# Feeding the first modulation of a two-block diffusion layer: VectorE sums one shift vector, the adaptive loads start earlier, the second shift's matmuls move

## The chip, the cores and the metric

One core of one Trainium2 chip. The time is device microseconds for one execution, the median of the runs shown. All data is float32; the heavy products are made of three passes over high and low parts.

## What is computed

The part that matters is the beginning of the first block: six modulation vectors come out of one product of `silu(c)` (1 x 1024) with `ada_w` (1024 x 6144, 25.2 MB), and shift and scale enter the pooling mixer.

```python
def modulate(h, shift, scale):
    return h * (1 + scale) + shift

def ada_mods(cond, w, b):
    mods = (jax.nn.silu(cond) @ w + b)[..., None, :]
    return jnp.split(mods, ADA_CHUNKS, axis=-1)

# first_block
sh1, sc1, g1, sh2, sc2, g2 = ada_mods(c, ada_w[i], ada_b[i])
u = modulate(rms_norm(x, mix_pre_g[i]), sh1, sc1)
y = pool_mixer(u, pool_w[j], pool_scale[j])      # (window mean - u) @ w, four groups of 256
x = x + g1 * rms_norm(y, mix_post_g[i])
f = conv_ffn(modulate(rms_norm(x, ffn_pre_g[i]), sh2, sc2), ...)
x = x + g2 * rms_norm(f, ffn_post_g[i])
```

After it come the feed-forward block and a second block (two linear-attention mixers), which the change doesn't touch.

## The kernel before

The kernel is written by hand in five streams, one for each engine, that are kept in step by named semaphores. x (512 x 1024) lies as four token tiles in `xres`. Everything before the first feed-forward product takes about 79 us; then TensorE runs products until the end.

**The adaptive weights.** `ada_w` is read in 24 units of 1 MB: unit u = 4j + n holds the rows 256n to 256n + 255 of vector j (0 shift, 1 scale, 2 gate, 3 second shift, 4 second scale, 5 second gate). They pass through six slots (`ADA_SLOTS`). SyncE's `ada_unit` issues them in the order of u, from line 333 on, with `pool_w` (two halves of 512 KB) behind unit 7 and the first feed-forward weights (`unit(0, ...)`, line 339) behind unit 13. Ahead of unit 0 it waits until x has landed (line 332); from unit 6 on it waits until TensorE has used the unit that held the slot (`ada_used`). TensorE's `ada_unit(j, n)` (line 1791) multiplies a unit by the columns of `c_col` in four column groups of 32, so that each of the four partial sums has one row group of a bank. `ada_sum(j)` on VectorE (line 1087) copies the bank to `ada_part`, and `mod_col` on TensorE (line 1807) adds the partial sums and turns the vector into a column for every block of 128 channels; `mod_col` on VectorE (line 1100) adds the bias. The last vector, the second gate, goes another way: VectorE's `gate_sum` (line 1226) adds 128 x 1024 products into `g2_acc` with one SCALAR_TENSOR_TENSOR for each k, and a matmul with ones adds over the partitions.

**Order on TensorE, lines 1782 to 1940.** `keep_busy(14, 2)`, four turns of the small rows, the rows of `pool_scale` and `mix_post_g` spread over the partitions (line 1879), `keep_busy(2, 4)`, the band sums (line 1889, 16 matmuls), units 0 and 1, `pool_block(0)` to `(3)` (line 1839: the window means of the normed x), units 2 and 3, `pool_block(4)` to `(7)`, `mod_col(0)`, units 4 to 7, `mod_col(1)`, unit 8, then the mixer product tile by tile: `mixed(0)` with the units 9 to 11 between its groups, `mixed(1)` with `mod_row(2, 0)` behind its first group, `mixed(2)`, `mixed(3)`; then units 12 to 15, `turn_normed(0)`, the first half of `mod_col(3)`, units 16 and 17, `turn_normed(1)`, the second half, units 18 and 19, `turn_normed(2)`, `mod_col(4)`, `turn_normed(3)`, `keep_busy(6, 3)` and the first feed-forward product (line 291).

**Order on ScalarE, lines 559 to 630.** `Silu` for `c_col`, four square sums of x, a square root, the four normed tiles (line 567), the eight `pooled` copies (571), the eight scalings with SC1 (575), then square sums and roots of y and of the new x tile by tile. The copy of vector 3's partial sums (line 611) stands behind `norm_scale(1)`.

**Order on VectorE, lines 1061 to 1172.** Four copies for `edge_band`, four copies of columns behind `c_silu`, `pool_scale_row` and `post1_row` (1077, 1079), the inverse root, `band_sums` (1085), `ada_sum(0)`, `mod_col(0)`, `ada_sum(1)`, `mod_col(1)`; then for cb = 0 to 7 `scale_weights` at cb 0 and 4 (1137) and one SCALAR_TENSOR_TENSOR each (1149), which writes what the mixer reads; `ada_sum(2)`, the gate row (1154) and the four tiles of norm, scaling and addition.

Of the kernel before, what the change touches and what calls it, by code (L numbers as in the profile page):

```python
# [69 lines left out]
def build(nc, a, out, debug=None):  # L70
# [53 lines left out]
    vec_rows = at("vec_rows", PH + 24 * KB, [D])  # L124
# [85 lines left out]
    with ExitStack() as ctx:  # L210
# [88 lines left out]
        def _(sp):  # L299
# [32 lines left out]
            sp.wait_ge(S("x_in"), 16 * TT)  # L332
# [138 lines left out]
        def _(act):  # L471
# [100 lines left out]
            act.wait_ge(S("mods_done"), 2)  # L572
# [35 lines left out]
            act.wait_ge(S("ada_used"), 16)  # L608
            act.wait_ge(S("mod_mm"), 2)
            act.wait_ge(S("ada_summed"), 3)  # L610
# [418 lines left out]
        def _(v):  # L1029
# [37 lines left out]
            v.wait_ge(S("rows_turned"), 1)  # L1067
            v.wait_ge(S("c_silu"), 1)
            V.tensor_copy(bgk_norm[:], ps[:, 6, KD:KD + LH + DV // P]).then_inc(S("cols_done"), 1)
            V.tensor_copy(conv_taps[:].rearrange("p a n -> p (a n)"), ps[:, 7, 16:16 + 8 * FC]).then_inc(S("cols_done"), 1)  # L1070
            V.tensor_copy(gdn_taps[:].rearrange("p a n -> p (a n)"), ps[:, 7, 16 + 8 * FC:16 + 8 * FC + P]).then_inc(S("cols_done"), 1)

            v.wait_ge(S("rows_turned"), 1)
            V.tensor_copy(cond_cols[:].rearrange("p a k -> p (a k)"), ps[:, 6, 14:62]).then_inc(S("cols_done"), 1)
            v.wait_ge(S("cols_done"), 4)
            v.wait_ge(S("vec_mm"), 1)
            V.tensor_copy(pool_scale_row[:], bank2(2)).then_inc(S("vec_done"), 1)
            v.wait_ge(S("vec_mm"), 2)
            V.tensor_copy(post1_row[:], bank2(0)).then_inc(S("vec_done"), 1)
# [7 lines left out]
            def ada_sum(j):  # L1087

                v.wait_ge(S("ada_used"), 4 * j + 4)
# [5 lines left out]
                else:  # L1095
                    if j == 4:
                        v.wait_ge(S("ada_summed"), 4)
# [1454 lines left out]
```

## Time and profile before

| | |
|---|---|
| median of 3 runs | 1148.26 us (1147.45 to 1153.53) |
| span of the profiled execution | 1146.0 us |
| TensorE busy | 1128.1 us (98%) |
| VectorE, ScalarE, GpSimd busy | 551.4, 503.3, 450.0 us |
| granted TensorE clock, mean | 0.995 |
| first feed-forward product starts | 79.08 us |

The one time that the trace gives for the profiled execution is its span, from the first to the last instruction; what lies around it is in the median alone, which is 2.3 us above. In the profile a matmul of float32 stands as several passes, so counts of TensorE lines are passes; "L291" is line 291; a queue's name with q (SPq, ACTq) is the issuing of its transfers; the bracket at a row's end is the engine's idle time just before it and what ended it.

### The profile page before, as it was taken

How to read it: one execution, taken by the hardware profiler on the slowest of the kernel's cores; microseconds unless marked ns; L12 is line 12 of the kernel's file. 1: busy time of each engine (PE TensorE's matmuls, PEld its weight loads, DVE VectorE, ACT ScalarE, POOL GpSimd, SP SyncE). 2: the span in 40 equal slices, each digit the busy share in tenths (PEclk: the TensorE clock that was granted, in tenths of full speed). 3: DMA queues.
4: the chain of work that ended last, by engine and by line, in shares of the span. 5: the costliest groups of instructions: out<-in, count | busy, mean ns of one | idle time of the engine just before them, and what ended most of it. 6: DMA issues, size and time to landing. Idle time of an engine off the chain costs nothing.

```text
span 1146.0 us, 17133 instructions
## 1 busy us (share of the span) xinstructions
PE 1128.1 (98%) x6818; PEld 920.9 (80%) x6818; DVE 551.4 (48%) x907; ACT 503.3 (44%) x701; POOL 450.0 (39%) x340
## 2 busy tenths in 40 slices
PE   9999999999999999999999999999999999999997
PEld 6568888888888888878788878888888888888886
DVE  2472554334452234577986655422200443676836
ACT  4474553544421223865443245745322343534632
POOL 0015544445455471654442311034454534564430
PEclk9899999999999999999999999999999999999999
DMA  9994232332342333424232211222243322323201
GB/s 347 413 360 132 74 110 77 106 110 73 110 126 79 110 110 112 148 86 136 74 88 98 74 37 38 74 74 74 96 137 110 110 79 82 103 75 112 74 1 74
DMA packets 86216, 128.97 MB, mean 113 GB/s; under 512 B 13300, under 2 KB 66306, under 8 KB 85895
## 3 DMA queue, kind: packets, MB, share of 16 engines
q1 hardware_dynamic: 80706, 119.62, 30.9%
q10 hardware_dynamic: 5445, 8.42, 2.1%
q8 instruction: 48, 0.79, 0.3%
q14 instruction: 17, 0.14, 0.0%
HBM read 122.77 MB, written 5.26 MB: 112 GB/s over the span
## 4 chain that ended last, share of the span: by engine, by line
PE 88%; DVE 6%; ACT 3%; DMA 1%; issue 1%; SPq 0%; POOL 0%; DVEq 0%; ACTq 0%; POOLq 0%
PE ps L291 24%; PE ps L293 23%; PE ps L292 23%; PE ps L1773 3%; DVE conv_v L1291 2%; PE ps L1854 1%; PE ps L1803 1%; PE ps L2244 1%; DVE diag L1352 1%; PE ps L2245 1%; PE ps L1779 1%; PE ps L2313 1%; PE ps L2303 1%; PE ps L2250 1%; DVE outer L1349 1%
## 5 line engine op out<-in xcount | busy, mean ns | idle before, releaser
L426 POOL TENSOR_TENSOR wl<-raw,wh 128x512 fp32r<-128x512 f32 x312 | 419.4, 1376 | 615.6 <-ACT wh L477 615.6
L291 PE MATMUL ps<-xth,wh 128*128 128x512 f32 (+1 forms) x832 | 324.6, 390 | 1.5 <-DVE xtl L1188 0.9
L293 PE MATMUL ps<-xth,wl 128*128 128x512 f32 (+1 forms) x832 | 317.5, 382 | 0.0
L292 PE MATMUL ps<-xtl,wh 128*128 128x512 f32 (+1 forms) x832 | 317.2, 381 | 0.0
L477 ACT ACTIVATE wh<-raw 128x2048 fp32r<-128x2048 f32 x78 | 149.3, 1914 | 303.9 <-PE ps L293 281.9
L291 PEld LDWEIGHTS ps<-xth,wh 128*128 128x128 f32 x832 | 156.5, 188 | 34.7 <-issue 4.4
L293 PEld LDWEIGHTS ps<-xth,wl 128*128 128x128 f32 x832 | 156.4, 188 | 30.4
L292 PEld LDWEIGHTS ps<-xtl,wh 128*128 128x128 f32 x832 | 156.7, 188 | 28.8 <-issue 0.5
L1196 DVE SCALAR_TENSOR_TENSOR conv_out<-ps,conv_taps,conv_out 128x511 f32<-128x511 f32 x44 | 32.8, 744 | 124.8 <-ACT conv_out L644 124.8
L1291 DVE SCALAR_TENSOR_TENSOR conv_v<-ps,gdn_taps,conv_v 128x511 f32<-128x511 f32 (+2 forms) x96 | 71.8, 748 | 38.2 <-ACT conv_v L712 35.5
L291 PE MATMUL ps<-wh,xth 128*128 128x512 f32 x176 | 69.7, 396 | 0.1
L293 PE MATMUL ps<-wh,xtl 128*128 128x512 f32 x176 | 68.5, 389 | 0.0
L292 PE MATMUL ps<-wl,xth 128*128 128x512 f32 x176 | 68.5, 389 | 0.0
L291 PE MATMUL ps<-wh,act_parts_h 128*128 128x512 f32 x160 | 62.4, 390 | 0.0
L293 PE MATMUL ps<-wh,act_parts_l 128*128 128x512 f32 x160 | 62.3, 389 | 0.0
L292 PE MATMUL ps<-wl,act_parts_h 128*128 128x512 f32 x160 | 62.2, 389 | 0.0
L1610 DVE SCALAR_TENSOR_TENSOR xres<-xres,ps 128x1024 f32<-128x1024 f32 x7 | 8.5, 1220 | 90.5 <-PE ps L293 90.5
L712 ACT ACTIVATE conv_v<-ps,gdn_taps 128x512 f32<-128x512 f32 x32 | 21.9, 683 | 54.7 <-PE ps L293 29.9
L291 PE MATMUL ps<-wh,ogt_h 128*128 128x512 f32 x112 | 43.8, 391 | 0.0
L293 PE MATMUL ps<-wh,ogt_l 128*128 128x512 f32 x112 | 43.6, 389 | 0.0
L292 PE MATMUL ps<-wl,ogt_h 128*128 128x512 f32 x112 | 43.6, 389 | 0.0
L1222 DVE CAST act_parts_h<-acts 128x512 fp32r<-128x512 f32 x20 | 9.9, 495 | 65.3 <-PE ps L293 65.3
(350 smaller groups left out, 1644.9 us busy)
## 6 DMA issues: line engine op xcount, KB each, us to landing
ada<-in_ada_w SPq DMA_DIRECT2D x24, 1024.0 KB, 11.3
raw<-in_gdn_w_in SPq DMA_DIRECT2D x24, 1024.0 KB, 5.2
raw<-in_ffn_w_up SPq DMA_DIRECT2D x22, 1024.0 KB, 4.9
raw<-in_gla_w_in SPq DMA_DIRECT2D x12, 1024.0 KB, 5.0
raw<-in_ffn_w_down SPq DMA_DIRECT2D x11, 1024.0 KB, 4.9
raw<-in_gdn_w_out SPq DMA_DIRECT2D x8, 1024.0 KB, 4.9
raw<-in_gla_w_out SPq DMA_DIRECT2D x4, 1024.0 KB, 5.0
xres<-in_x SPq DMA_DIRECT2D x4, 512.0 KB, 4.9
```

Of the source, the lines that this page charges most:

```text
L291: nc.tensor.matmul(o, lh, rh, start=first, stop=False)
L292: nc.tensor.matmul(o, lh, rl, start=False, stop=False)
L293: return nc.tensor.matmul(o, ll, rh, start=False, stop=last)
L426: rest = nc.gpsimd.tensor_tensor(lo[:, part], raw[:, s, part], hi[:, part].bitcast(f32), ALU.subtract)
L477: nc.scalar.activation(wh[:, s if w is None else w, :], raw[:, s, :], ACT.Copy).then_inc(hi_done, 1)
L712: nc.scalar.activation(conv_v[:, sub, :], ps[:, piece_bank(piece), :], ACT.Copy, scale=gdn_taps[:, 3, ch:ch + 1]).then_inc(S("tap3"), 1)
L1196: V.scalar_tensor_tensor(dst[:, 1:T], src[:, 0:T - 1], conv_taps[:, 0, ds(chunk, 1)], dst[:, 1:T], ALU.mult, ALU.add).then_inc(S("conv_lef ...
L1291: V.scalar_tensor_tensor(dst[:, j:T], src[:, 0:T - j], gdn_taps[:, 3 - j, ch:ch + 1], dst[:, j:T], ALU.mult, ALU.add)\
L1349: V.tensor_tensor(prod, diag[:, 0:j, j:j + 1].broadcast_to([P, j, n]), diag[:, j:j + 1, j + 1:32].broadcast_to([P, j, n]), ALU.mult).then_ ...
L1352: V.tensor_tensor(diag[:, 0:j, j + 1:32], diag[:, 0:j, j + 1:32], prod, ALU.add).then_inc(S("diag_done"), 1)
L1773: return X.transpose(o, x, ident[0:n, 0:n])
L1779: X.matmul(ps[:, b, 0:256], ones[:, 0:1].broadcast_to([P, P]), group_rows[:, 0:1].broadcast_to([P, 256]), start=True, stop=True)
```

## The change

- VectorE makes the first shift vector: `shift_sum(k)` multiplies a unit's half by `c_col[k]` and adds it into `shift_acc` (one TENSOR_SCALAR and seven SCALAR_TENSOR_TENSOR of 128 x 1024), and `shift_col` on TensorE adds over the partitions with eight matmuls of one column. TensorE's units 0 to 3, `ada_sum(0)` and their `mod_col(0)` are gone.
- SyncE no longer waits for x ahead of unit 0. Units 6 to 9 wait for `shift_summed`, later ones for `ada_used`, whose count is four lower. `unit(0, ...)` goes two units earlier.
- The turned rows share bank 0; `Silu` stands behind the first two square sums; the band sums come ahead of the spread rows on TensorE, `keep_busy(2, 4)` is gone, all eight `pool_block` follow each other, and then come units 4 to 7.
- VectorE's order is inverse root, `band_sums`, the two spread rows, the eight `shift_sum`, `scale_weights(0)`, `ada_sum(1)`, the scale column, the shift column. ScalarE scales with SC1 as soon as the scale column is there.
- TensorE calls `keep_busy(2, 7)` ahead of `mod_col(1)` and again behind `shift_col`. Unit 12 goes ahead of `mixed(2)`, unit 13 between its groups; units 14 and 15 stay behind `mixed(3)`.

```diff
-            sp.wait_ge(S("x_in"), 16 * TT)
...
-                if u >= ADA_SLOTS:
-                    sp.wait_ge(S("ada_used"), u - ADA_SLOTS + 1)
+                if u >= ADA_SLOTS + 4:
+                    sp.wait_ge(S("ada_used"), u - ADA_SLOTS - 3)
+                elif u >= ADA_SLOTS:
+                    sp.wait_ge(S("shift_summed"), 2 * (u - ADA_SLOTS) + 2)
...
-            for u in range(8, 14):
+            for u in range(8, 12):
                 ada_unit(u)
             unit(0, (0, w_up[0, 0]))
-            for u in range(14, 20):
+            for u in range(12, 20):
...
-            act.wait_ge(S("rows_turned"), 1)
-            nc.scalar.activation(c_col[:], ps[:, 6, 0:KD], ACT.Silu).then_inc(S("c_silu"), 1)
             for tt in range(TT):
                 act.wait_ge(S("x_in"), 16 * TT)
+                if tt == TT // 2:
+                    act.wait_ge(S("rows_turned"), 1)
+                    nc.scalar.activation(c_col[:], ps[:, 0, 0:KD], ACT.Silu).then_inc(S("c_silu"), 1)
                 square_sum(junk[:], xres[:, tt, :], stat[:, 0, tt:tt + 1])
...
-            act.wait_ge(S("mods_done"), 2)
+            act.wait_ge(S("mods_done"), 1)
...
+            def shift_sum(k):
+
+                u = k // 2
+                v.wait_ge(S("c_silu"), 1)
+                if k % 2 == 0:
+                    v.wait_ge(ada_full[u], 16)
+                if k == 0:
+                    V.tensor_scalar(shift_acc[:], ada[:, u, 0, :], c_col[:, 0:1], None, ALU.mult).then_inc(S("shift_summed"), 1)
+                else:
+                    v.wait_ge(S("shift_summed"), k)
+                    V.scalar_tensor_tensor(shift_acc[:], ada[:, u, k % 2, :], c_col[:, k:k + 1], shift_acc[:], ALU.mult, ALU.add)\
+                        .then_inc(S("shift_summed"), 1)
...
-            ada_sum(0)
-            mod_col(0, 2, SH1)
...
+            vector_rows()
+            for k in range(KD):
+                shift_sum(k)
+            scale_weights(0)
             ada_sum(1)
             mod_col(1, 3, SC1, PRE1)
+            mod_col(0, 2, SH1)
             v.wait_ge(S("mods_done"), 2)
-            v.wait_ge(S("cols_done"), 8)
             for cb in range(KD):
-                if cb % 4 == 0:
-                    scale_weights(cb // 4)
+                if cb == KD // 2:
+                    scale_weights(1)
...
+            def shift_col(b):
+
+                pe.wait_ge(S("shift_summed"), KD)
+                for k in range(KD):
+                    mm = X.matmul(ps[:, b, k:k + 1], shift_acc[:, k * P:(k + 1) * P], ones[:, 0:1], start=True, stop=True)
+                mm.then_inc(S("mod_mm"), 1)
+
+            pe.wait_ge(S("cols_done"), 8)
+            for cb in range(KD):
+                pool_block(cb)
             pe.wait_ge(S("vec_done"), 2)
-            ada_unit(0, 0)
-            ada_unit(0, 1)
-            pe.wait_ge(S("cols_done"), 8)
-            for cb in range(4):
-                pool_block(cb)
-            ada_unit(0, 2)
-            ada_unit(0, 3)
-            for cb in range(4, KD):
-                pool_block(cb)
-            mod_col(0, 2, 0)
-            mod_col(0, 2, 1)
             for n in range(4):
                 ada_unit(1, n)
+            pe.wait_ge(S("pooled_done"), KD)
+            keep_busy(2, 7)
             mod_col(1, 3, 0)
             mod_col(1, 3, 1)
+            shift_col(2)
+            keep_busy(2, 7)
             ada_unit(2, 0)
-            pe.wait_ge(S("pooled_done"), KD)
...
+            def second_shift(g):
+
+                if g == 1:
+                    ada_unit(3, 1)
+
             mixed(0, gate_unit)
             mixed(1, gate_row)
-            mixed(2)
+            ada_unit(3, 0)
+            mixed(2, second_shift)
             mixed(3)
-            for n in range(4):
-                ada_unit(3, n)
+            ada_unit(3, 2)
+            ada_unit(3, 3)
```

## Rows read from the trace of the kernel before

**Rows 1.** The page's first line

```profile
span 1146.0 us, 17133 instructions
```

**Rows 2.** The chain that ended last, 0 to 130 us: start, length, what

```profile
22.39 4.09 PE ps L1839 x32
...
53.03 9.50 PE ps L1854 x44
62.53 1.90 PE ps L1803 x16
64.44 7.28 DMA ada<-in_ada_w
```

**Rows 3.** Timeline of TensorE, 50 to 86 us

```profile
67.10 0.43 PE L1813 MATMUL ps<-group_rows,ada_part 128*32 128x1 f32 x32
...
71.76 1.06 PE L1803 MATMUL ps<-ada,c_col 128*32 128x512 f32 x8 [0.18 <-DMA ada<-in_ada_w]
...
75.35 2.78 PE L1779 MATMUL ps<-group_rows,ones 128*128 128x256 f32 x12
```

**Rows 4.** Timeline of ScalarE, 50 to 90 us

```profile
59.11 1.02 ACT L501 ACTIVATE junk<-ps 128x1024 f32<-128x1024 f32 x1 [0.82 <-PE ps L1854]
...
66.47 0.58 ACT L611 ACTIVATE ada_part<-ps 128x512 f32<-128x512 f32 x1
```

**Rows 5.** Windows: stretch, length, busy time (count) by engine, PEclk, DMA share, GB/s

```profile
35.00:38.50 3.50, 2.16 (x80) 0.89 (x72) 1.11 (x4) 0.09 (x1) 0.00 (x0) 1.00 1.03 416
38.50:42.00 3.50, 2.82 (x10) 1.03 (x11) 3.50 (x5) 3.50 (x6) 0.00 (x0) 0.51 1.03 421
42.00:45.40 3.40, 3.40 (x11) 1.90 (x14) 3.40 (x6) 1.43 (x3) 0.00 (x0) 0.50 1.02 418
```

**Rows 6.** Timeline of all engines, 0 to 125 us: ScalarE's part of it

```profile
6.71 1.28 ACT L560 ACT_TABLE_LOAD   x1 [6.71 <-issue]
...
12.17 1.05 ACT L501 ACTIVATE junk<-xres 128x1024 f32<-128x1024 f32 x1
...
17.06 1.28 ACT L509 ACT_TABLE_LOAD   x1
...
18.80 4.27 ACT L567 ACTIVATE xn<-xres,stat 128x1024 f32<-128x1024 f32 x4 [0.24 <-DVE stat L1050]
```

**Rows 7.** Timeline of ScalarE in the feed-forward loop, 100 to 118 us

```profile
105.59 1.28 ACT L477 ACT_TABLE_LOAD   x1
```

**Rows 8.** Timeline of all engines, 0 to 125 us: VectorE's part of it

```profile
15.22 1.21 DVE L1079 COPY post_row<-ps 128x1024 f32<-128x1024 f32 x1
...
18.80 2.48 DVE L1085 COPY band_sum<-ps 128x512 f32<-128x512 f32 x4
```

**Rows 9.** The source line of `gate_sum`

```profile
L1235 DVE SCALAR_TENSOR_TENSOR g_acc<-ada,c_col,g_acc x8: 1276/1285/1289, 132.8 to 157.7; 128x1024 f32<-128x1024 f32 x8
```

**Rows 10.** Timeline of SyncE's queue, 0 to 130 us

```profile
9.33 13.49 SPq L326 DMA_DIRECT2D ada<-in_ada_w  x8
```

**Rows 11.** The tile `ada`, 0 to 110 us: its transfers

```profile
DMA to landing us min/median/max: 5.1/11.3/15.9
```

**Rows 12.** The tile `pool_w`, 0 to 50 us: its transfers

```profile
L336 SPq DMA_DIRECT2D pool_w<-in_pool_w x1: 507/507/507, 23.4 to 23.4; - x1
...
DMA to landing us min/median/max: 11.3/11.8/12.4
```

**Rows 13.** Timeline of VectorE, 33 to 48 us

```profile
36.49 0.69 DVE L1098 COPY ada_part<-ps 128x512 f32<-128x512 f32 x1 [3.27 <-PE ps L1803]
...
38.41 1.22 DVE L1137 TENSOR_TENSOR pool_w<-pool_w,pool_scale_row 128x1024 f32<-128x1024 f32 x1
39.56 2.74 DVE L1149 SCALAR_TENSOR_TENSOR pooled<-band_sum,mod_cols,pooled 128x512 f32<-128x512 f32 x4
```

**Rows 14.** Timeline of TensorE, 33 to 52 us

```profile
37.23 0.71 PE L1813 MATMUL ps<-group_rows,ada_part 128*32 128x1 f32 x64 [0.79 <-DVE ada_part L1098]
38.63 1.93 PE L1803 MATMUL ps<-ada,c_col 128*32 128x512 f32 x8 [0.69 <-DMA ada<-in_ada_w]
41.11 3.75 PE L1854 MATMUL ps<-pool_w,pooled 128*128 128x256 f32 x8 [0.55 <-ACT pooled L575]
```

More of the change, by code:

```diff
@@ L1107, in mod_col @@
                     V.scalar_tensor_tensor(out, ps[:, b, 0:KD], 1.0, bias, ALU.add, ALU.add).then_inc(S("cols_done"), 1)
-                    v.wait_ge(S("cols_done"), 9 if which == SC1 else 12)
+                    v.wait_ge(S("cols_done"), 10 if which == SC1 else 12)
                     V.tensor_tensor(out, out, cond_cols[:, gain, :], ALU.mult).then_inc(S("mods_done"), 1)
@@ L1126, in turned_out @@
                               bank2(turned_bank(tt)).rearrange("p (k n) -> p k n", n=P)).then_inc(S("pooled_written"), 1)
-            inv_root(stat[:, 0, 0:TT], D, EPS, TT)
-            band_sums()
-            ada_sum(0)
-            mod_col(0, 2, SH1)
             def scale_weights(part):
@@ L1785, in _ @@
             pe.wait_ge(S("ident_in"), 16)
-            turn(ps[:, 6, 0:62], rows[0:62, 0, :], 62)
-            turn(ps[:, 7, 16:16 + 4 * FC], rows[0:4 * FC, 1, :], 4 * FC)
-            turn(ps[:, 7, 16 + 4 * FC:16 + 8 * FC], rows[0:4 * FC, 2, :], 4 * FC)
-            turn(ps[:, 7, 16 + 8 * FC:16 + 8 * FC + P], rows[:, 3, :]).then_inc(S("rows_turned"), 1)
+            turn(ps[:, 0, 0:62], rows[0:62, 0, :], 62)
+            turn(ps[:, 0, 64:64 + 4 * FC], rows[0:4 * FC, 1, :], 4 * FC)
+            turn(ps[:, 0, 64 + 4 * FC:64 + 8 * FC], rows[0:4 * FC, 2, :], 4 * FC)
+            turn(ps[:, 0, 64 + 8 * FC:64 + 8 * FC + P], rows[:, 3, :]).then_inc(S("rows_turned"), 1)
             def ada_unit(j, n):
@@ L1794, in ada_unit @@
                 pe.wait_ge(ada_full[u % ADA_SLOTS], 16 * (u // ADA_SLOTS + 1))
-                if n == 0 and j >= 2:
-                    pe.wait_ge(S("ada_summed"), j - 1)
-                    if j >= 3:
-                        pe.wait_ge(S("mods_done"), 3)
+                if n == 0 and j >= 3:
+                    pe.wait_ge(S("ada_summed"), j - 2)
+                    pe.wait_ge(S("mods_done"), 3)
                 for b in range(2):
@@ L1874, in turn_normed @@
                 turn_tile(xn[:, tt, :], turned_bank(tt))
-            pe.wait_ge(S("prepared"), 8)
-            for r, b in ((0, 2), (32, 0)):
-                for half in range(2):
-                    mm = X.matmul(ps[:, b + half, :], ones[r:r + 1, 0:1].broadcast_to([1, P]), vec_rows[r:r + 1, half * 512:half * 512 + 512],
-                                  start=True, stop=True)
-                mm.then_inc(S("vec_mm"), 1)
-            pe.wait_ge(S("c_silu"), 1)
-            pe.wait_ge(S("cols_done"), 4)
-            keep_busy(2, 4)
             pe.wait_ge(S("band_in"), 20)
@@ L1891, in _ @@
                 mm.then_inc(S("pool_mm"), 1)
-            pe.wait_ge(S("vec_done"), 2)
-            ada_unit(0, 0)
-            ada_unit(0, 1)
-            pe.wait_ge(S("cols_done"), 8)
-            for cb in range(4):
-                pool_block(cb)
-            ada_unit(0, 2)
-            ada_unit(0, 3)
-            for cb in range(4, KD):
-                pool_block(cb)
-            mod_col(0, 2, 0)
-            mod_col(0, 2, 1)
+            for r, b in ((0, 2), (32, 0)):
+                if r:
+                    pe.wait_ge(S("c_silu"), 1)
+                    pe.wait_ge(S("cols_done"), 4)
+                for half in range(2):
+                    mm = X.matmul(ps[:, b + half, :], ones[r:r + 1, 0:1].broadcast_to([1, P]), vec_rows[r:r + 1, half * 512:half * 512 + 512],
+                                  start=True, stop=True)
+                mm.then_inc(S("vec_mm"), 1)
+            def shift_col(b):
[6 more added lines that the diff above has]
+                pool_block(cb)
+            pe.wait_ge(S("vec_done"), 2)
             for n in range(4):
                 ada_unit(1, n)
+            pe.wait_ge(S("pooled_done"), KD)
+            keep_busy(2, 7)
             mod_col(1, 3, 0)
             mod_col(1, 3, 1)
+            shift_col(2)
+            keep_busy(2, 7)
             ada_unit(2, 0)
-            pe.wait_ge(S("pooled_done"), KD)
             def gate_unit(g):
@@ L1964, in _ @@
             pe.wait_ge(S("mods_done"), 5)
-            pe.wait_ge(S("ada_summed"), 5)
+            pe.wait_ge(S("ada_summed"), 4)
             up_units(0)
```

38 lines of the change are left out of this document (20 added, 18 removed).

## The prediction

> **What bounds the kernel now.** I read the page first: a span of 1146.0 us [rows 1], TensorE busy for 98% of it. From 79.08 us on, products of three passes follow each other and nothing that the change touches is in them, so the change is worth what it moves the moment 79.08, with its sign turned, and no more. The profiled span is 2.3 us below the median of 1148.26 us; I work out a shift against the span's clock and add it to the median.
>
> Then the chain of waits. It seems to give the answer at once: 7.28 us from 64.44 to 71.72 belong to the landing of an adaptive unit [rows 2]. The reader should not take that for a stall of 7.28 us. TensorE's timeline shows the unit used at 71.76 after 0.18 us of idleness [rows 3]; until then it had work that could not go earlier. That work began at 67.10 with the second shift's first half column, which needs `ada_part`, and ScalarE writes it in 66.47 to 67.05, behind its whole row of square sums and roots [rows 4]. That row is fed at 59.11 by a square sum that had waited 0.82 us for the mixer product: `mixed(2)` ends there, since seven groups at 9.50 / 11 = 0.86 us from 53.03 make 59.07 [rows 2, 4]. So the line that sets the end is: scale column, mixer product up to the end of `mixed(2)`, the ScalarE and VectorE row up to 67.05, units 16 to 19 and three turns, 79.08. The last transfer is beside it, 0.2 us late.
>
> The third view is the granted clock: 1.0 from 35 to 38.5 us with TensorE busy for 2.16 of 3.5, then 0.5 (the 1.2 GHz level) until 45.4, although it was busy for 2.82 of 3.5 and 3.40 of 3.40 [rows 5]. A unit's eight passes took 1.93 us there [rows 14] against 0.95 at full clock (16 in 1.90 [rows 2]).
>
> **The change, part by part.**
>
> *The start.* ScalarE can begin its square sums when x is there, 9.33 us, where SyncE's wait ends now [rows 10], instead of 12.17 [rows 6]. Two take 2.5 us, to 11.8. Then comes `Silu`. Now one table load stands ahead of it at 6.71 where nothing waits, and the square sums use the same table. Which table a kernel that starts with a square sum loads first, the trace doesn't show, but its feed-forward loop does show the pattern: a plain copy (line 477) loads a table that doesn't serve the Gelu after it, so each pass loads twice [rows 7]. I take it that the first square sum loads such a common table and `Silu` needs a second load in the middle: 1.28 us, bounds 0 and 1.28. `Silu` ends at 13.3, the square sums at 15.8 instead of 17.05, and with the second load of 1.28 the normed tiles begin at 17.6 instead of 18.80: 1.2 us gained. The Trainium skill (ScalarE: Activation LUTs, What ACT_TABLE_LOAD costs) prices a switch at 2.66 us, as a load and a drain of 1.38; by it the gain would be gone. The trace has the load at 17.06 for 1.28 us and its root right behind it, so I use the row [rows 6].
>
> *The transfers.* Without the wait unit 0 follows x directly, and units 0 to 5 are in by about 25 us. But unit 6 now waits for VectorE's second `shift_sum`. VectorE does `band_sums` (2.48 us) from 17.6 to 20.1 and two row copies of 1.2 us to 22.5 [rows 8]. The eight sums cost 1.285 us each in `gate_sum` [rows 9], 1.31 with the wait on themselves; the first is a TENSOR_SCALAR, bounded by 0.6 and 1.3, taken as 1.1. The second ends at 24.9, the fourth at 27.5, the eighth at 32.7. **So the shift vector is not summed as the units land, but as VectorE comes free.** Unit 6 is issued at 24.9 and lands 5.1 us later at the earliest [rows 11], at 30.0. At the 2.5 us for 1.05 MB that 416 GB/s make [rows 5], unit 7 is in at 32.5 and `pool_w` at 35.1. Now its second half, issued at 23.4, lands 11.8 us later, at 35.2 [rows 12]. The early start of the stream is lost in the gap behind unit 5. Behind `pool_w` nothing starves: unit 11 lands at 45, unit 13 at 53, unit 19 at 68, some 4 us ahead of now, which frees the 0.2 us of [rows 3].
>
> *The scale column.* `scale_weights(0)` stands ahead of `ada_sum(1)` and needs `pool_w`: 35.1 to 36.3. `ada_sum(1)` then ends at 37.0; now it ends at 37.18, and scaling starts at 38.4 [rows 13]. So the scale vector comes first in the order, but 0.2 us earlier in time. The 3.8 us of units 0 to 3 that TensorE no longer works are not on this line.
>
> *The shift column and the mixer.* What moves is the 1.2 us of `scale_weights(0)` [rows 13], which is over before SC1, and in its place stands `shift_col`. It is sixteen passes with 128 columns of weights and one of output. Bounds: `mod_col`'s 64 passes took 0.71 us [rows 14], 0.2 us for sixteen; `pool_block`'s passes, with as many weights and 144 columns, took 4.09 / 32 = 0.13 [rows 2], 2.0 us for sixteen, and twice that at half clock, 4.1. Between these I take 1.3 us, since the weights are the dear side's and the output the cheap side's. TensorE is at 37.7 after `mod_col(1)`, at 39.0 after `shift_col`; VectorE's mixing products begin at 39.3 (39.56 now [rows 13]). Then TensorE has four passes of `keep_busy` (0.93 us at 2.78 / 12 [rows 3], 1.85 at half clock) and unit 8, which now runs in 38.63 to 40.56 while scaling goes on. `mixed(0)` begins at 40.9 at full clock, at 42.8 at half; now at 41.11 [rows 14]. Which clock? TensorE here idles more of the stretch ahead of 38.5 than it does now, and now the clock falls; once down it stayed there until 45.4 [rows 5]. I take the half clock, so `mixed(0)` is 1.7 us late. Its first two groups and half-clock tail repeat what now costs 3.75 us, but some of the delay is made up: 45.4 finds it in its second group, and from there on it is at full speed and doesn't wait for VectorE. Worked out group by group (two at half clock from 42.8 to 45.6, then two groups, three units and `mixed(1)`'s first group at 0.95 to 1.05 each) the gate row starts at 51.6 and 53.03 becomes 53.3: 0.3 us late. At full clock throughout the same count gives 51.1, 1.9 us early. With the dearest `shift_col` it is 2.0 us late; if the clock comes back at 42 instead of 45.4, 1.7 us early.
>
> *Units 12 and 13.* They cost 2 x 0.95 = 1.9 us [rows 2]. Now they run after 62.53, where TensorE would otherwise wait for 67.05. The change puts unit 12 ahead of `mixed(2)` and unit 13 in it, and the end of `mixed(2)` is on the line that sets the end: 59.07 becomes 59.07 + 0.3 + 1.9 = 61.3. The hole they leave ahead of 67 is filled by nothing. This is the largest term, a loss of 1.9 us, and the change gains only if the mixer starts more than that early.
>
> *The rest.* From the second tile's square sum on, everything is shifted; unit 19's 0.2 us come back. The first feed-forward unit lands 5 us earlier, and it is not late now.
>
> **The sum**: 0.3 + 1.9 - 0.2 = 2.0 us later. The median becomes 1148.26 + 2.0 = **1150.2 us**.
>
> **The rivals.**
>
> *The clock holds.* The two `keep_busy` calls keep 2.4 GHz over the mixer's start. For: that is work just where the clock falls. Against: 0.93 us each, when 2.16 in 3.5 did not hold it [rows 5]. The term is -1.9 instead of 0.3, with the other two -0.2: 1148.1 us. If in addition `Silu` shares the first table, 1.3 us more: 1146.8. Together 22%.
>
> *The chain's transfer is a true stall.* Then a last unit that lands 4 us earlier moves 79.08 by nearly that: 1148.26 - 3.7 = 1144.6. For it speaks the chain [rows 2], against it the 0.18 us [rows 3]. 8%.
>
> *The hole at 65 us.* TensorE, done with units 14 and 15, turns a tile and then waits some 1.5 us for `ada_part`. If that brings the clock down, units 16 to 19 and the turns run at half: four units at 0.98 more and two of the turns' 1.0, about 4 us on top: 1154.2, slower. [...] 12%. The Trainium skill (TensorE: Matmul & The Clock Gate, Part 4: PE-mode transpose) says that a transpose doesn't count as busy; by that rule this rival would be likelier. No row shows it.
>
> *The change doesn't do what it says at its start.* The adaptive units, now right behind x, share the transfer engines with the small rows and `pool_band`; band sums start late, VectorE with them, unit 6 with VectorE. With 2 us there: 1152.2. Against: the small rows compete with x already. 8%.
>
> The rest, 50%, is the forecast, with its bounds 1148.3 (the clock back at 42) and 1152.0 (the dearest `shift_col`).
>
> **How the numbers follow.** The forecast's own bounds, the clock rival and the late start make 1146.8 to 1152.2; that leaves out the transfer rival and the clock's fall at 65 us. Range 1146.5 to 1153.0. A measurement of this kernel tells about 0.5% (5.7 us) from no change: under 1142.5 or over 1154.0. No case reaches the first except a sum of the best ones, 3%; the hole's 1154.2 lies on the second, and half of it with a little for mishaps makes 7%; same 90%.
>
> **What would show it.** Right: a second table load ahead of `Silu` near 11.8; first `shift_sum` near 22.5, with units 0 to 3 long landed; a gap in the transfers near 25 us; `ada_sum(1)` ending near 37; clock 0.5 from about 38.5 to 45; `mixed(2)` ending near 61.3, line 611's copy near 69, no wait for unit 19, and the first product near 81. Wrong: full clock over 38 to 45; a first product before 79; a clock below 1.0 after 60; or a span that differs from that moment's shift, for then something in the later stages answers to the earlier transfers.

## The result and the profile after

The changed kernel takes 1156.70 us (median of 6 runs, 1154.00 to 1158.28) against 1148.12 us of the kernel before (6 runs): a ratio of 1.0075, with a 95% interval of 1.0063 to 1.0087. It is slower, 8.6 us by the medians. The forecast was 1150.2 us with a range of 1146.5 to 1153.0: the sign was right, the size four times too small, and the result outside the range. It also lies above 1154.0 us, which the forecast had given 7%.

The profiled execution has a span of 1152.4 us and a time of 1154.18 us. The page's first line and its row of busy times:

```profile
span 1152.4 us, 16995 instructions
...
PE 1126.2 (98%) x6742; PEld 920.7 (80%) x6742; DVE 559.4 (49%) x914; ACT 504.2 (44%) x702; POOL 450.1 (39%) x340
```

The span is 6.4 us longer than in [rows 1], and the first feed-forward product starts at 85.87 instead of 79.08, 6.8 us later. In both kernels 1066.5 to 1066.9 us lie between that product and the end, so the loss is all made before it. Where, the chain that ended last tells; its part up to 42 us, with start, length and what it was:

```profile
5.62 10.13 DMA pool_band<-in_pool_band
16.76 5.99 PE ps L1897 x32
22.75 1.92 PE ps L1905 x8
...
25.84 1.21 DVE post_row L1082
27.05 0.67 DVE shift_acc L1091
27.83 1.30 DVE shift_acc L1094
29.25 1.29 DVE shift_acc L1094
30.63 1.30 DVE shift_acc L1094
32.87 7.09 DMA pool_w<-in_pool_w
39.99 1.22 DVE pool_w L1149
41.21 0.61 DVE ada_part L1114
```

Read it from below. The scale vector's `ada_sum(1)` waits on VectorE's queue behind the scaling of `pool_w` (39.99); `pool_w` was issued at 32.87, because its transfer stands on SyncE's queue behind unit 7, and unit 7 waits for the fourth `shift_sum`, which ends at 31.9; the sums start at 27.0, because the band sums and two row copies are ahead of them on VectorE, and the copies wait for the spread rows (L1905), which the change put behind the band matmuls (L1897) on TensorE; and the band matmuls are late because `pool_band`, issued at 5.62, took 10.13 us to land. Before it took 4.9. From the first sum on, the prediction had every link of this chain. Of the part ahead of it, it put the late landing aside as a rival of 8%, and it had no wait of VectorE for TensorE: it took the band sums and the copies as following the normed tiles.

TensorE's timeline from 37 to 90 us, as far as it answers to [rows 2, 3, 14]: start, length, instruction, idle time before and its releaser.

```profile
41.87 0.71 PE L1830 MATMUL ps<-group_rows,ada_part 128*32 128x1 f32 x64 [2.48 <-DVE ada_part L1114]
42.51 1.95 PE L1913 MATMUL ps<-ones,shift_acc 128*128 128x1 f32 x16
44.32 1.80 PE L1797 MATMUL ps<-group_rows,ones 128*128 128x256 f32 x4
46.04 1.94 PE L1820 MATMUL ps<-ada,c_col 128*32 128x512 f32 x8
47.91 2.03 PE L1871 MATMUL ps<-pool_w,pooled 128*128 128x256 f32 x8
...
55.94 1.90 PE L1839 MATMUL ps<-ada_part,group_rows 128*128 128x512 f32 x4
...
74.28 0.43 PE L1830 MATMUL ps<-group_rows,ada_part 128*32 128x1 f32 x32 [1.69 <-ACT ada_part L614]
...
85.87 0.47 PE L292 MATMUL ps<-xth,wh 128*128 128x512 f32 x1 [0.95 <-DVE xtl L1206]
```

With VectorE's copy for the scale vector at 41.13 (36.49 in [rows 13]) and the gate row, `mod_row`, at 55.94 (51.13 before), the 6.8 us are three terms:

| stretch | before | after | forecast | measured |
|---|---|---|---|---|
| up to the copy of `ada_part` (scale) | 36.49 | 41.13 | -0.2 | +4.6 |
| from there to `mod_row` | 14.64 | 14.81 | +0.5 | +0.2 |
| from `mod_row` to the first product | 27.95 | 29.93 | +1.9, less 0.2 | +2.0 |

The medians differ by 8.6 us, more than the traces. The changed kernel's mean clock was 0.995 in the profiled run and 0.989 to 0.993 in the other five, whose spans ran from 1152.2 to 1156.5 us; the kernel before had 0.993 to 0.998 in the runs beside the experiments. So the change also makes the clock lower in most runs; the profiled run is one of its best, with as much half clock as the profile before (10.2 us in all), at other places.

### The profile page after: what moved, and what is told of

Its sections match the earlier page's. It is cut to its first block, busy times and chain, and to the rows that moved or that the text cites. A ratio compares the mean times of both kernels' runs of the same rounds, so it can differ in the third digit from the quotient of the medians.

```text
span 1152.4 us, 16995 instructions
## 1 busy us (share of the span) xinstructions
PE 1126.2 (98%) x6742; PEld 920.7 (80%) x6742; DVE 559.4 (49%) x914; ACT 504.2 (44%) x702; POOL 450.1 (39%) x340
## 4 chain that ended last, share of the span: by engine, by line
PE 84%; issue 5%; POOL 4%; DVE 3%; ACT 2%; DMA 1%; ACTq 0%; DVEq 0%; SPq 0%; POOLq 0%
PE ps L292 23%; PE ps L293 23%; PE ps L294 23%; POOL wl L428 3%; PE ps L1791 3%; PE ps L1871 1%; PE ps L2269 1%; PE ps L2270 1%; PE ps L1820 1%; DMA pool_band<-in_pool_band 1%; PE ps L2338 1%; POOL attn L452 1%; PE ps L2328 1%; PE ps L2275 1%; PE ps L2455 1%
## 5 line engine op out<-in xcount | busy, mean ns | idle before, releaser
L292 PEld LDWEIGHTS ps<-xth,wh 128*128 128x128 f32 x832 | 156.5, 188 | 34.9 <-issue 3.7
```

The source lines that it names most:

```text
L292: nc.tensor.matmul(o, lh, rh, start=first, stop=False)
```

## The experiments

Everything below is told against the kernel before, run on the same chip; "first product" is the start of the first feed-forward product in the profiled run, and half-clock stretches are read from its granted clock.

**One part at a time: the wait for x.** The changed kernel with SyncE's wait put back, and the kernel before with only that wait taken out.

```
 for tt in range(TT):
     sp.dma_start(xres[:, tt, :], ...)
+sp.wait_ge(S("x_in"), 16 * TT)        # a1_x_wait; b1_no_x_wait: the reverse, in the kernel before
 for u in range(8):
```

> The changed kernel with SyncE's wait for x ahead of unit 0 put back. Theory A (the late small transfers are the cause: with the adaptive units right behind x, pool_band landed at 15.8 us instead of 10.6, and the band sums, VectorE's row and the second half of the adaptive stream all hang on it): pool_band lands at 10.6, the first shift_sum starts near 22.5 instead of 27.0, the gap in the transfers near 27 to 33 us is gone, and the first feed-forward product starts at about 81 instead of 85.9, so some 4.8 us less than the changed kernel and 2 us more than before. Theory B (the cost is in what was moved and in the clock, and the early stream is neutral): within 1 us of the changed kernel, 85 to 87, since the stream itself starts 2 us later.

> The kernel before with only the wait for x ahead of unit 0 taken out. Theory A: pool_band lands near 15.8 here too, the small rows near 13.5, the band sums start near 17 instead of 15.1, and the scale column, behind pool blocks and units 4 to 7 on TensorE, comes 1 to 3 us later: first product at 80 to 82 instead of 79.1. Theory B: a stream that starts 2 us earlier costs nothing, first product at 78 to 79.1.

Measured: with the wait back 1152.2 us, 1.0041 (1.0025 to 1.0058), first product 84.56; without it in the kernel before 1152.35 us, 1.0041 (1.0027 to 1.0055), first product 82.60, 3.5 us late. By the times, taking the one line out costs the kernel before 0.41%, and putting it back lowers the ratio of the changed kernel from 1.0075 (1.0094 in a second measurement below) to 1.0041. The timeline of all engines at the start of the kernel before without the wait:

```profile
13.55 0.68 PE L1772 MATMUL ps<-ident,rows 62*128 62x62 f32 x4 [2.00 <-DMA vec_rows<-in_mix_post_g]
15.71 0.43 DVE L1061 COPY edge_band<-pool_band 128x512 f32<-128x512 f32 x1 [15.71 <-DMA pool_band<-in_pool_band]
```

One removed line moves `pool_band` from 10.61 to 15.71 and the turns of the small rows from 11.38 to 13.55; the changed kernel has 15.77 and 13.57. Nothing else of the change is needed for it. With the wait back in the changed kernel `pool_band` is there at 10.93, and the first `shift_sum` starts at 22.43, the moment that the prediction named (22.5). But the scale column stays late. VectorE's timeline of that kernel:

```profile
22.43 0.74 DVE L1092 TENSOR_SCALAR shift_acc<-ada,c_col 128x1024 f32<-128x1024 f32 x1
...
37.03 1.23 DVE L1150 TENSOR_TENSOR pool_w<-pool_w,pool_scale_row 128x1024 f32<-128x1024 f32 x1 [4.05 <-DMA pool_w<-in_pool_w]
38.17 0.69 DVE L1115 COPY ada_part<-ps 128x512 f32<-128x512 f32 x1
```

The units now start at 9.83 and not at 3.54, so `pool_w` has them ahead of it on the wire and lands at 37.0, and the half clock, from 40.2 for 6.8 us, lies over `shift_col` and the mixer's start (`shift_col` 3.01 us, first product 84.6 and not near 81). So the expectation held for the landing, the first sum and the gap in the transfers (375 GB/s from 25 to 30 us), and missed on the first product. The early stream and the early small rows can't both be had by this edit: the wait buys one with the other.

**One part at a time: units 12 and 13.** The changed kernel with them behind `mixed(3)` as before, and the kernel before with them moved.

```
-ada_unit(3, 0)
-mixed(2, second_shift)
+mixed(2)
 mixed(3)
-ada_unit(3, 2)
-ada_unit(3, 3)
+for n in range(4):                     # a2_units_back; b2_units_between: the reverse, in the kernel before
+    ada_unit(3, n)
```

> The changed kernel with units 12 and 13 back behind mixed(3). Theory A and the prediction's largest term: mixed(2) ends 1.9 us earlier, ScalarE's and VectorE's row with it, first product at 84.0 instead of 85.9. Rival (the row is held by something else, and the two units fill idle time): no change, 85.9.

> The kernel before with only the change's place for units 12 and 13 (ahead of mixed(2) and between its groups). The prediction's term: mixed(2) ends at 61.0 instead of 59.1 and the first product starts at 81.0 instead of 79.1, 1.9 us slower; unit 18 is issued some 6 us earlier and nothing comes of it. Rival (the last transfer is a true stall of several us): the first product starts earlier than 79.1.

Measured: put back, 1152.53 us, 1.0042 (1.003 to 1.0055); moved in the kernel before, 1148.47 us, 1.0006 (0.9997 to 1.0016). The stretch from `mod_row` to the first product is the clean measure, since no half clock lies in it: 27.54 with the units back (86.31 - 58.77) against 29.93, and 29.93 with them moved (80.27 - 50.34) against 27.95. The term is 2.0 to 2.4 us; the prediction had 1.9. The stretch is 29.93 us in every other profile with the moved units but one, too. The first product of the kernel with the units put back is itself a miss, 86.31 and not 84.0: its half clock lay over the mixer's start, from 41.5 for 10.2 us. TensorE's rows of the kernel before with the units moved show the hole they leave:

```profile
57.68 1.06 PE L1803 MATMUL ps<-ada,c_col 128*32 128x512 f32 x8
58.67 5.45 PE L1854 MATMUL ps<-pool_w,pooled 128*128 128x256 f32 x24
...
65.91 1.09 PE L1773 MATMUL ps<-ident,xn 128*128 128x128 f32 x8
68.69 0.43 PE L1813 MATMUL ps<-group_rows,ada_part 128*32 128x1 f32 x32 [1.69 <-ACT ada_part L611]
```

The time of the moved kernel is up by less than the term: 1.2 us by the medians (1147.25 beside it), 0.7 by the ratio. Its profile points to the clock: the half-clock stretch at the mixer was 3.4 us long and not 6.8, and `mod_row` 0.8 us early; the first product was 1.2 us late. And the kernel with the units put back gained more in its times (1.0042 against 1.0075 and 1.0094) than the 2.4 us; what the rest is, no trace shows.

**The changed kernel once more.** To see how much of the trace repeats.

> The changed kernel once more, for a second profile. Its profiled run (span 1152.4, mean clock 0.995) was its second best; the others reach 1156.5 at 0.989 to 0.993, while the kernel before stays at 0.995 to 0.998. Theory C (the 1.5 us hole ahead of the second half column, forecast at 65 and seen at 72.6 to 74.3, lets the clock fall in other runs): the profile of a run with a clock of 0.991 has a stretch at half clock between 66 and 86 us. Theory D (the lower clock is the same two places as in the first profile, the idle start and the mixer's start, with longer stretches): half clock only before 55 us, about 20 us of it.

Measured: 1157.57 us, 1.0094 (1.0077 to 1.0111), first product 86.33. The start repeats to about 1 us (`pool_band` at 14.93, the copy of `ada_part` at 39.92), but the clock fell in other places, one of them the hole. TensorE's row behind it, and two windows (stretch, length, busy time by engine, PEclk, DMA share, GB/s):

```profile
73.38 3.47 PE L1820 MATMUL ps<-ada,c_col 128*32 128x512 f32 x16
```

```profile
70.00:73.90 3.90, 2.21 (x48) 1.28 (x48) 2.59 (x5) 3.61 (x8) 0.00 (x0) 0.96 1.06 396
73.90:77.40 3.50, 3.50 (x21) 1.12 (x14) 2.08 (x6) 2.67 (x8) 0.00 (x0) 0.56 1.03 421
```

Sixteen passes take 3.47 us instead of 1.92. That is the rival of the hole at 65 us: it happened in this execution and not in the first one, and cost 1.6 us, not 4, since the clock came back after 3.4 us. The same wait of 1.7 us ahead of the second half column stands in the profiles of a1_x_wait, b2_units_between, a3_pool_w_early and d1_band_first, and in none of them did the clock fall there: one profile in six.

**`pool_w` ahead of the waiting units.** On top of the wait for x, `pool_w` is issued behind unit 5.

```
-for u in range(8):
+for u in range(6):
     ada_unit(u)
 sp.dma_start(pool_w[:, 0:2], ...)
 sp.dma_start(pool_w[:, 2:4], ...)
+for u in range(6, 8):
+    ada_unit(u)
```

> With the wait for x put back and pool_w issued behind unit 5 instead of behind unit 7. Theory A2 (with the start mended, the landing of pool_w is what VectorE's scale_weights(0), and behind it the scale column, wait for: 4.05 us idle until 37.03 us): scale_weights(0) runs at 33.0, right behind the last shift_sum, and the copy of the scale vector's sums at 36.5 to 37.2 instead of 38.17, now held by unit 7; 1 to 1.7 us gained on a1_x_wait. Rival (the copy was bound by TensorE's units all along): no gain.

Measured: 1151.65 us, 1.0037 (1.0025 to 1.005), first product 82.57. `pool_w` is scaled at 33.16 right behind the sums, and no wait is left there; the scale column, at 37.64, waits for TensorE's units instead (3.26 us on VectorE). The column came a little later than the 36.5 to 37.2 expected; the first product gained 2.0 us on a1_x_wait, where 1 to 1.7 were expected. What is left against the kernel before is the 2.0 us of the units 12 and 13 and 1.5 us ahead of `mod_row` (52.64).

**The three causes together.** The wait for x back, `pool_w` behind unit 5, units 12 and 13 back; the first shift vector stays with VectorE, the scale vector's column stays first.

> The changed kernel with the wait for x, pool_w behind unit 5 and units 12 and 13 behind mixed(3). If the three found causes make up the loss: first product at 80.5 to 81.5 (a3_pool_w_early's 82.6 less 2.0), total within 0.2% of the kernel before. Rival (something else is left): above 82.

Measured: 1148.45 us, 1.001 (1.0001 to 1.0019, 11 runs), first product 79.05 where the kernel before has 79.08. TensorE's rows of this kernel:

```profile
42.76 2.33 PE L1874 MATMUL ps<-pool_w,pooled 128*128 128x256 f32 x8
...
51.49 1.90 PE L1842 MATMUL ps<-ada_part,group_rows 128*128 128x512 f32 x4
```

So these three make up the loss to within 0.1% (the interval leaves out zero), and the rest of the change, the sum on VectorE and the new order around it, gains nothing. The first product came 1.5 us ahead of the expected 80.5 to 81.5; in this execution the half clock lay at 18.6 to 25.4 and not over the mixer, and with full clock there `mod_row` is still 0.4 us later than in the kernel before.

**Is `pool_band` alone the late one?** In the changed kernel its transfer goes first on ScalarE's queue.

```
+act.dma_start(pool_band[:]...).then_inc(S("band_in"), 16)
 act.dma_start(rows[KD:KD + LH, 0, :], ...)
...
 act.dma_start(vec_rows[32:33, :], a["mix_post_g"]).then_inc(S("rows_in"), 16)
-act.dma_start(pool_band[:]...).then_inc(S("band_in"), 16)
```

> The changed kernel with pool_band issued first on ScalarE's queue instead of last but two. Theory A in its detail (ScalarE's queue of small rows gets a small share of the transfer engines while SyncE's queue is full, so what is last on it is late): pool_band lands before 8 us, the turns, behind the small rows, at 14 instead of 13.6, band sums start at 14.6 instead of 16.8, first shift_sum at about 25, first product 2 us earlier than 85.9 (less what the clock gives or takes). Rival (the bytes of pool_band are what is slow, wherever it stands): the small rows come later by what pool_band comes earlier, turns at 16 and no gain.

Measured: 1155.77 us, 1.0062 (1.0042 to 1.0082). `pool_band` is there at 3.70, and yet the turns wait for `vec_rows` until 14.00 and the first sum starts at 25.65, only 1.3 us early; half clock from 40.6 for 10.2 us ate that (first product 87.62). So it is not `pool_band` alone that is late: with it out of the way the small rows behind it, each of few bytes, still hold the turns. A version that holds the units back only for the small rows, and not for x, was not run.

**More work where the clock falls.** The changed kernel with more `keep_busy` at four places, one of them the hole; then the hole's alone.

```
-keep_busy(14, 2)
+keep_busy(18, 2)                       # a4_more_busy
...
+keep_busy(5, 2)                        # a4_more_busy, behind the turns
...
-keep_busy(2, 7)
+keep_busy(7, 7)                        # a4_more_busy, ahead of mod_col(1)
...
 turn_normed(0)
+pe.wait_ge(S("x1_done"), 3)
+keep_busy(3, 3)                        # a4_more_busy and e1_hole_busy
 mod_col(3, 1, 0)
```

> The changed kernel with more keep_busy where TensorE idles: 18 instead of 14 at the start, 5 ahead of the band sums, 7 instead of 2 ahead of the scale column, 3 in the hole behind turn_normed(0). Theory (idle stretches bring the clock down; the fall costs the band sums 2 us and the mixer's start 1.7 us): no half clock at 14.6 to 21.4 and none at 45 to 52, mean clock 0.997 or more, first product near 82.5 instead of 85.9. Rival (the late landings alone set the pace): under 1 us of gain, with a full clock.

> The changed kernel with three keep_busy matmuls in the hole behind turn_normed(0) and nothing else. Theory C (the second profile of the changed kernel had half clock from 74.0 to 77.4, its first had not; the hole lets the clock fall in most runs and costs 1.6 us there): no half clock between 66 and 86, from the gate row to the first product 29.9 us in every profile, and the median 1 to 2 us below the changed kernel's. Rival (the fall comes from the start and the mixer's start alone): median unchanged, clocks of 0.989 to 0.992 as before.

Measured: all four places 1152.01 us, 1.0046 (1.0029 to 1.0063), mean clocks of 0.997 and 0.998, first product 82.87; the hole alone 1156.83 us, 1.008 (1.0068 to 1.0092), clocks 0.989 to 0.993, as without it. The first kernel is 5.6 us better than the changed one on the same chip (1157.57), though it still has the late small rows and the moved units; only one half-clock stretch is left (23.9, 3.4 us long). Its `pool_band` landed at 15.66, as late as before, but with full clock over the band matmuls the first sum started at 24.95 and not at 26.97. In the second the rival came true: its hole was full and its clock stayed up there, but it fell for 10.2 us over the mixer's start. TensorE's rows of the kernel with the hole alone filled:

```profile
41.30 1.04 PE L1830 MATMUL ps<-group_rows,ada_part 128*32 128x1 f32 x64 [2.43 <-DVE ada_part L1114]
42.26 3.57 PE L1913 MATMUL ps<-ones,shift_acc 128*128 128x1 f32 x16
...
49.55 2.72 PE L1871 MATMUL ps<-pool_w,pooled 128*128 128x256 f32 x8
...
74.77 1.47 PE L1797 MATMUL ps<-group_rows,ones 128*128 128x256 f32 x6
76.61 0.43 PE L1830 MATMUL ps<-group_rows,ada_part 128*32 128x1 f32 x32 [0.38 <-ACT ada_part L614]
```

The same sixteen passes of `shift_col` take 3.57 us here and 1.95 in the first trace of the changed kernel. Half clock over the band matmuls, for 6.8 us, is in both profiles; what this execution has more than the first is all between 41 and 51 us, where TensorE has just waited 2.4 us for the late scale column.

**All mends and all the filling.** The three causes mended, the `keep_busy` of above, and one more edit: a `Silu` ahead of the square sums, so that no activation table is loaded between them.

```
+nc.scalar.activation(glast_exp[:, 0, 0:1], ones[:, 0:1], ACT.Silu)      # its result is not used
 for tt in range(TT):
     act.wait_ge(S("x_in"), 16 * TT)
```

> All mends together: wait for x back, pool_w behind unit 5, units 12 and 13 behind mixed(3), the keep_busy calls of a4_busy, and one Silu of one column at the start, so that no table load stands between the square sums. Theory A with all its terms: first shift_sum near 21.2, scale column's copy near 36, first product at 77 to 78, 1 to 2 us better than the kernel before. Rival (VectorE's shift sums cost what TensorE saved): at 79 or later, no better than before.

Measured: 1154.82 us, 1.0069 (1.0052 to 1.0085), first product 84.17 where 77 to 78 was expected: the largest miss. VectorE's rows:

```profile
33.29 1.22 DVE L1153 TENSOR_TENSOR pool_w<-pool_w,pool_scale_row 128x1024 f32<-128x1024 f32 x1
38.45 0.69 DVE L1118 COPY ada_part<-ps 128x512 f32<-128x512 f32 x1 [3.94 <-PE ps L1826]
42.91 0.17 DVE L1127 SCALAR_TENSOR_TENSOR mod_cols<-ps,cond_cols 128x8 f32<-128x8 f32 x1 [3.77 <-PE ps L1836]
```

TensorE's `keep_busy(7, 7)` began at 38.31 in a half-clock stretch and took 3.90 us; `mod_col(1)` stood behind it, and VectorE waited 3.77 us. In a4_more_busy the same filling ended at 39.64, when `mod_col(1)` became ready. So here a fixed count of filling was not free: it would have been only if the wait had been as long as the filling at half clock. The `Silu` edit did what it should (the later `Silu` starts at 12.71 with no load ahead of it), but nothing came of it at the first sum, which started at 22.82, since the row copies waited 1.14 us for TensorE, where five `keep_busy` matmuls had been put ahead of the spread rows; what it is worth alone is not shown.

**The idea of the change without its costs.** The kernel before with the scale vector's units first on the wire, the shift vector's units behind them summed by VectorE as they land, the x wait, `pool_w` and units 12 and 13 as before; then the same with more filling ahead of `shift_col`.

```
-sp.dma_start(ada[:, u % ADA_SLOTS], ada_v[u // 4, u % 4])
+sp.dma_start(ada[:, u % ADA_SLOTS], ada_v[1 - u // 4 if u < 8 else u // 4, u % 4])
...
 mod_col(1, 3, 0)
 mod_col(1, 3, 1)
+keep_busy(4, 7)                        # c1_scale_first; 9 in c2_scale_busy
+pe.wait_ge(S("shift_summed"), KD)
+for k in range(KD):
+    mm = X.matmul(ps[:, 2, k:k + 1], shift_acc[:, k * P:(k + 1) * P], ones[:, 0:1], start=True, stop=True)
```

> The kernel before, with its wait for x, its start and its units 12 to 15, but with the scale vector's units first on the wire (TensorE uses them from 20 us on, in the places of units 0 to 3) and the shift vector's behind them, summed by VectorE as they land at 25 to 33 us. If what failed in the changed kernel is only where the sums stand (ahead of pool_w and of the scale column, in a stream that waits for them): scale column at 33 to 34 instead of 38.4, all shift sums done near 35.5 to 36, shift column near 38.5, mixer products done by 44.5 instead of 46.1, gate row at 48 to 49 instead of 51.1 and the first product at 76 to 77.5 instead of 79.1; 2 to 3 us faster than before. Rival (any sum on VectorE costs what TensorE saves, since the mixer waits for VectorE's eight products): 79 or later.

> c1_scale_first with keep_busy(9, 7) instead of (4, 7) between mod_col(1) and the shift column, so that TensorE works through 32.6 to 37.2 us. If the clock alone ate c1's gain (half clock from 37.1 to 47.3; shift column 3.57 us instead of 1.95, mixer's start at half): clock full from 20 to 50, shift column done at 39.4, mixed(0) from 40.4, gate row at 48.5 to 49, first product at 76.5 to 77, total 0.15 to 0.25% below the kernel before. Rival (nine matmuls don't hold the clock, or run at half and hold up the shift column): first product at 80 or later.

Measured: 1147.26 us, 0.9998 (0.9989 to 1.0007), first product 80.56; with more filling 1147.35 us, 0.9997 (0.9988 to 1.0006), first product 78.78. VectorE's rows of the second:

```profile
26.33 0.75 DVE L1093 TENSOR_SCALAR shift_acc<-ada,c_col 128x1024 f32<-128x1024 f32 x1 [5.80 <-DMA ada<-in_ada_w]
...
34.72 0.17 DVE L1127 TENSOR_TENSOR mod_cols<-mod_cols,cond_cols 128x8 f32<-128x8 f32 x1
...
39.56 0.17 DVE L1123 TENSOR_TENSOR mod_cols<-ps,cond_cols 128x8 f32<-128x8 f32 x1 [0.90 <-PE ps L1931]
39.76 2.74 DVE L1173 SCALAR_TENSOR_TENSOR pooled<-band_sum,mod_cols,pooled 128x512 f32<-128x512 f32 x4
```

The scale column is done at 34.9, some 3.5 us ahead of the kernel before, where scaling began at 38.4. Nothing comes of it, since the mixing products need the shift column too, and that is done at 39.7; they begin at 39.76, against 39.56 in [rows 13]. VectorE's eight sums run from 26.33 to 37.5, with the scale column's steps between them, and `shift_col` follows until 39.5: together they end no earlier than what they replace. Both expectations, a first product near 77, were missed. With more filling the clock fell at 40.0, for 3.4 us. With five `keep_busy` matmuls fewer it fell at 36.7 and stayed down for 10.2 us, and the first product was 1.8 us later; but the medians are the same, so that this too lies within what the clock changes from run to run. No version tried beats the kernel before; these two tie with it, and the one with the three mends is within 0.1%.

## Why the prediction was wrong, point by point

- **What bounds the kernel**: right. The change is worth what it moves the first product, and the chain's 7.28 us of transfer [rows 2] were no stall: in the changed kernel unit 19 was issued at 64.40, as before (64.44), and landed at 73.7, some 5 us ahead of its use, and nothing was gained by that. The later stages took 1066 to 1067 us in all kernels but one (a5_mends, with a half-clock stretch at 514 us, 1068.4).
- **The start**: wrong, and with it most of the miss. The forecast let the normed tiles and VectorE's band sums begin early (17.6) and the first `shift_sum` at 22.5. Measured: turns 13.57, band matmuls from 16.76, normed tiles 20.08, first sum 26.97. The step that failed is the one that priced the removed wait at a gain alone (1.2 us at the normed tiles). What the runs show in its place is a loss: taken out of the kernel before, the wait costs 3.5 us at the first product and 0.41% in time (b1_no_x_wait). About 2.0 of the 4.5 us at the first sum are the half clock over the band matmuls, which TensorE ran in a stretch at 1.2 GHz (13.9 to 20.7), after waits of 2.5 us for the small rows and 2.3 for `pool_band`; filled there, it let the sums start at 24.95 (a4_more_busy). The forecast had no TensorE link there at all, neither these matmuls nor the spread rows behind them. The rival had the mechanism, small rows and `pool_band` sharing the engines with the units, but at 8% and with 2 us; its argument against, that they compete with x already, was the error, because x ends at 9.3 and the units do not. [rows 10] held the answer: no unit was issued before 9.33, and `pool_band`, issued at 5.67, moved between 8 and 10.6, while x was ending and no unit had yet come.
- **The transfers**: the links held (second sum to unit 6, fourth sum to `pool_w`, a gap near 25 us), from a start 4.5 us late. The gap, in windows of the changed kernel (DMA share and GB/s are the last two columns):

```profile
25.00:30.00 5.00, 5.00 (x44) 5.00 (x44) 4.75 (x5) 2.71 (x5) 0.00 (x0) 1.00 0.03 9
30.00:35.00 5.00, 4.91 (x45) 2.87 (x44) 4.52 (x5) 2.07 (x4) 0.00 (x0) 1.00 0.94 303
```

  From 25 to 30 us, 9 GB/s. The first sum cost 0.74 us where 1.1 was taken. That unit 19 would land some 4 us earlier was wrong, as said above.
- **The scale column**: forecast 0.2 us early, measured 4.6 late; nearly all of it inherited from the start (4.5). The forecast left itself no room here: `pool_w` was at 35.1 and what it should not delay at 37.0, so anything late by more than a little passed through in full.
- **The shift column and the mixer**: the term was right (0.2 us against 0.5), its parts were not. `shift_col` took 1.95 us at full clock, the dear bound and not the 1.3 chosen: 0.12 us for each pass with one column of output, against 0.13 for `pool_block`'s with as many weights and 144 columns [rows 2]. The half clock came from 44.6 to 48.0, 3.4 us, and not from 38.5 to 45. A dearer `shift_col` and a shorter half clock nearly made up for each other, so the agreement of the sum is luck.
- **Units 12 and 13**: right, 2.0 us against 1.9.
- **The table load**: right in kind, and by the row. A second load of 1.28 us stands ahead of `Silu`, and nothing follows it but `Silu`:

```profile
14.57 1.28 ACT L565 ACT_TABLE_LOAD   x1 [2.65 <-PE ps L1791]
```

  `Silu` begins at 15.86, 14.57 + 1.28 + 0.01, so the drain of 1.38 us that the Trainium skill adds (ScalarE: Activation LUTs, What ACT_TABLE_LOAD costs) does not show here, nor behind the load at 17.06 in [rows 6], whose root starts at 18.35.
- **The rivals**: the clock did not hold over the mixer's start (in a4_more_busy it did, and that kernel, with its other fillings, was 5.6 us better). In the hole the clock fell in one profile of six; that rival's own terms, four units at 0.98 and two turns at 1.0, come to 5.9 us and not 4, and the measured cost was 1.6. What was missing among the rivals is the sum of the late start and a long half-clock stretch behind it. In the first trace of the changed kernel both falls followed waits of TensorE of 2.5 us for something late; filling such waits took away most of the half clock in a4_more_busy, not all.
- **The range** followed from pricing each rival alone on top of the forecast; with the late start at the measured 4.8 us (-0.2 to +4.6) instead of 2 that rival alone would have stood at 1155.0. The 1.7 us from there to the measured 1156.7 are about what the medians differ by more than the traces (8.6 against 6.8), the clock of the other runs.

## What to carry to other kernels

A wait ahead of a large stream may be there for nothing that its queue needs: before you take it out, list what the other queues have in flight at that moment, and who waits for the last of it. When a transfer is released by an engine's progress, follow the queue past it too: here `pool_w` waited for the fourth vector sum only because it stood behind a unit that did. A matmul put into an idle stretch to hold the clock stands ahead of what comes next, and delays it if that is ready sooner. And a vector that is ready earlier is worth something only if its partner is; the mixing products need both columns.

## What the runs showed of the hardware

**A queue of small pieces gets few bytes beside a queue of large ones.** Queues of the changed kernel from 8 to 10 and from 10 to 12 us: packets, MB, share of 16 engines. q1 carries x and the units, q10 ScalarE's small rows and `pool_band`.

```profile
q1 hardware_dynamic: 199, 0.75, 91.4%
q10 hardware_dynamic: 163, 0.07, 12.5%
...
q1 hardware_dynamic: 175, 0.66, 80.9%
q10 hardware_dynamic: 176, 0.15, 22.2%
```

And the kernel before from 8 to 10 us, when x's last pieces come until 9, and the first unit, issued at 9.33, has not begun to move:

```profile
q10 hardware_dynamic: 461, 0.47, 65.6%
q1 hardware_dynamic: 75, 0.24, 29.8%
```

Beside a full queue the small one moved 163 and 176 packets in 2 us, near the other's count, but 0.07 and 0.15 MB, because its packets hold 0.4 to 0.9 KB where the units' hold 3.8. With the other queue nearly empty it moved 461 packets and 0.47 MB. The counts of these two windows fit engines that serve the two queues in turn, whatever the pieces hold; that is inferred, not shown. For `pool_band`, behind the small rows on that queue, it went with 10.1 us to landing instead of 4.9. The Trainium skill (DMA: Bandwidth & Descriptors, Queues, rings and completion order) says that an engine goes round the queues that have work, a packet at a time, and gives a packet as several descriptors; the trace agrees with the turns, and doesn't show how many pieces make one.

**One-source and two-source operations on VectorE.** The first `shift_sum`, a TENSOR_SCALAR over 128 x 1024 float32 values in SBUF, took 0.74 us, and the SCALAR_TENSOR_TENSOR of the same size 1.285. The Trainium skill (VectorE: DVE Perf Modes, The perf-mode tier table) gives tensor_scalar on float32 in SBUF twice the rate of tensor_tensor, which has two sources, and has no row for SCALAR_TENSOR_TENSOR; the ratio here is 1.7.

**The clock's falls are not fixed to a place.** Two profiles of the changed kernel had half-clock stretches from 13.9 (6.8 us) and 44.6 (3.4), and from 15.6, 36.1, 42.9 and 73.6 (3.4 each). The first product was at 85.87 and 86.33. The spans of the other runs reach 3.5 us beyond these two (1156.5 against 1153.0); which falls those runs had stays open.
